# Gates as tanh, merge tiles ahead of the silu tiles, squares on VectorE and four modulation blocks on TensorE in a two-block kernel

## The reference

```python
z = rms_norm(x, norm_g) @ w_in            # 20 pieces, the last is mg: 4 x 1024 wide
y_a = fox_attention(...)                  # 8 heads, causal
y_b = rg_lru(xb, ...)                     # r, i = sigmoid(gates); a = exp(-8 r softplus(-lam)); scan
y_c = nsa_attention(...)                  # compressed, selected and window attention
y_d = spatial_gating(ud, vd, ...)
ys = [y_a * silu(ga), y_b * silu(gb), y_c * silu(gc), y_d * silu(gd)]
merged = sum_n sigmoid(mg[n]) * (ys[n] @ w_branch[n])
out = x + merged @ w_out
```

## Time and profile before

| | us |
|---|---|
| median of 3 runs | 1929.52 (1928.55 to 1930.72) |
| the profiled execution | 1932.03 |
| its span in the trace | 1930.3 |
| TensorE busy | 1719.5 (89%) |
| TensorE weight loads | 1457.5 (76%) |
| VectorE busy | 1350.7 (70%) |
| ScalarE busy | 901.9 (47%) |

### The profile page before, as it was taken

One profiled execution on the slowest core, in us unless ns is written; L12 is line 12 of the kernel. 1 busy time (PEld: TensorE's weight loads), 2 busy tenths in 40 slices (PEclk: granted clock), 3 DMA queues, 4 the chain that ended last, 5 costly groups with the idle time before them and its releaser, 6 DMA issues. The chain is left out here.

```text
span 1930.3 us, 26100 instructions
## 1 busy us (share of the span) xinstructions
PE 1719.5 (89%) x10016; PEld 1457.5 (76%) x10016; DVE 1350.7 (70%) x2526; ACT 901.9 (47%) x1535; POOL 48.4 (3%) x113
## 2 busy tenths in 40 slices
PE   2699998668999998988899898999997998999997
PEld 0578876456788886867688776888896887888987
DVE  7677873447799999867995477389964444655585
ACT  2533333625444442226464465333344575796741
POOL 0800000000000000000000000000000000000000
PEclk8799999879999998999999899999998989899999
DMA  7333331003222325653463101354554443433542
GB/s 278 128 131 110 131 128 47 1 33 131 70 95 88 106 91 176 218 165 101 158 209 130 55 1 66 110 166 152 154 187 142 148 147 121 121 121 112 161 144 98
DMA packets 65348, 237.93 MB, mean 123 GB/s; under 512 B 7183, under 2 KB 8648, under 8 KB 64968
## 3 DMA queue, kind: packets, MB, share of 16 engines
q1 hardware_dynamic: 64456, 234.69, 37.2%
q10 hardware_dynamic: 768, 1.58, 0.2%
HBM read 234.93 MB, written 1.05 MB: 122 GB/s over the span
## 5 line engine op out<-in xcount | busy, mean ns | idle before, releaser
L442 PE MATMUL banks<-m,weights_high 128*128 128x256 f32 (+1 forms) x4336 | 1050.5, 336 | 104.2 <-DVE m L871 45.1
L442 PEld LDWEIGHTS banks<-m,weights_high 128*128 128x128 f32 x4336 | 744.6, 194 | 201.5 <-DVE m L871 48.0
L442 PE MATMUL banks<-m,weights_low 128*128 128x256 f32 (+1 forms) x2168 | 720.3, 332 | 0.0
L474 DVE TENSOR_TENSOR weights_low<-weight_ring,weights_high 128x1024 fp32r<-128x1024 f32 x294 | 357.4, 1223 | 287.8 <-ACT weights_high L469 286.8
L442 PEld LDWEIGHTS banks<-m,weights_low 128*128 128x128 f32 x2168 | 420.6, 194 | 38.8
L469 ACT ACTIVATE weights_high<-weight_ring 128x1024 fp32r<-128x1024 f32 x294 | 310.2, 1056 | 283.6 <-PE banks L442 234.4
L591 DVE SCALAR_TENSOR_TENSOR m<-m,columns 128x189 f32<-128x189 f32 (+4 forms) x856 | 321.5, 452 | 22.6 <-ACT m L543 22.3
L716 DVE SCALAR_TENSOR_TENSOR m<-weight_ring,m 128x1024 bf16<-128x1024 f32 x192 | 234.7, 1223 | 16.4 <-DMA weight_ring<-in_weights 9.6
L542 ACT ACTIVATE m<-banks,columns 128x512 f32<-128x512 f32 (+1 forms) x120 | 83.3, 694 | 307.6 <-PE banks L442 307.4
L442 PE MATMUL banks<-m,weight_ring 128*128 128x256 f32 x704 | 155.2, 384 | 2.4 <-ACT m L833 2.4
L442 PEld LDWEIGHTS banks<-m,weight_ring 128*128 128x128 f32 x704 | 135.8, 193 | 21.8 <-ACT m L833 2.8
(11 more groups left out here) (363 smaller groups left out, 1629.1 us busy)
## 6 DMA issues: line engine op xcount, KB each, us to landing
weight_ring<-in_weights SPq DMA_DIRECT2D x434, 512.0 KB, 3.6
x<-in_tokens SPq DMA_DIRECT2D x1, 2048.0 KB, 14.3
m<-in_cmp_w SPq DMA_DIRECT2D x1, 2048.0 KB, 7.5
m<-in_cond SPq DMA_DIRECT2D x2, 512.0 KB, 4.9
out<-x SPq DMA_DIRECT2D x1, 1024.0 KB, 4.8
columns<-in_columns SPq DMA_DIRECT2D x1, 633.0 KB
m<-in_rg_w ACTq DMA_DIRECT2D x1, 512.0 KB, 4.5
m<-in_spatial_w ACTq DMA_DIRECT2D x1, 512.0 KB
```

The lines of the kernel that those rows point to most:

```text
L442: mm = pe.matmul(out, lhsT, rhs, start=p.start and i == 0, stop=p.stop and i == len(passes) - 1)
L474: dve.tensor_tensor(w_lo[:, g % PARTS, :], K.ring[:, PLACE[PRODUCT_BLOCKS[g]] % RING, :], w_hi[:, g % PARTS, :].bitcast(F32), ALU.subtract ...
```

## The change

- Setup: the first four mod0 blocks are laid out transposed and formed on TensorE as products of a 128x128 tile and two columns (`Modulator.sum`); they are spread among the other twelve in the stream. VectorE forms twelve blocks, then adds the bias to the four. A small transfer with the transposed conditions goes ahead of the others.
- Start of a stage: what VectorE makes first for `Normalise` (where the root is known before the stage) and `Split` goes ahead of the low parts of the weights (`vector_first`).
- `project2`: mg is emptied with Tanh (scale 0.5) instead of Sigmoid and comes ahead of ga: mg 35 to 66, ga 67 to 70, gb 71 to 74, gc 75 to 78, gd 79 to 82. The merge uses (tanh + 1) and a factor 0.5. The gates of the recurrence become Tanh as well, one item later; the scratch of the side branches moves to ga to gd. Attention results are stored to tiles of their own, and VectorE multiplies each silu tile when it is emptied. Attention pairs come every 7 ticks.
- The squares of the four sets go to VectorE. The key root becomes Ln and Exp, and each root and the forget logarithms load one table that holds both. Some slots move by one item.

```diff
+MOD_PE = 4
+SQUARES_AT = 2
-STREAM = blocks_of("mod0")[:MOD_FIRST] + blocks_of("even_in")[:TOGETHER] \
+STREAM = spread_among(blocks_of("mod0")[:MOD_PE], blocks_of("mod0")[MOD_PE:MOD_FIRST]) + blocks_of("even_in")[:TOGETHER] \
...
+            if prepare:
+                prepare.vector_first(dve)
             for g in range(begun, n_ahead):
                 low_part(dve, g)
...
+        sync.dma_start(self.turned, self.K.dram["cond_t"]).then_inc(*self.K.conds.up(16))
...
+    def sum(self, pe, b):
+        K, j = self.K, b - FIRST_TILE["mod0"] // TPB
+        pe.wait_ge(*K.silued.at(1))
+        wait_loaded(K, pe, PLACE[b])
+        for k in range(KD):
+            mm = pe.matmul(K.bank[:, 0, 2 * j:2 * j + 2], K.ring[:, PLACE[b] % RING, k * P:k * P + P],
+                           self.turned[:, k, :], start=k == 0, stop=k == KD - 1)
+        mm.then_inc(*K.mod_summed.up())
...
+            for b in on_tensor[:SQUARES_AT]:
+                modulator.sum(pe, b)
             pe.wait_ge(*ones.at(1))
             for k in range(KD):
                 sums.add(pe, k)
+            for b in on_tensor[SQUARES_AT:]:
+                modulator.sum(pe, b)
...
+            modulator.take_sums(dve, MOD_PE)
...
+        for name, branch in (("ga", self.attention.forgetting), ("gb", self.side.xc), ("gc", self.attention.selected),
+                             ("gd", self.f["ud"])):
+            j = item - self.item_of[name]
+            if 0 <= j < KB:
+                dve.wait_ge(*emptied)
...
+                gate = self.f[name][:, j, :]
+                dve.tensor_tensor(gate, gate, branch[:, j, :], ALU.mult)
...
-    BEGIN, SPACING = 62, 8
+    BEGIN, SPACING = 62, 7
...
-            dve.tensor_tensor(f[name][:, j, :], f[name][:, j, :], K.bank[:, self.OUT, 0:LAT],
-                              ALU.mult).then_inc(*self.gated.up())
+            kept = self.selected if branch else self.forgetting
+            dve.tensor_copy(kept[:, j, :], K.bank[:, self.OUT, 0:LAT]).then_inc(*self.stored.up())
...
-    KEYS, KEY_SQUARE, VALUES, KEY_SUM, KEY_ROOT, KEY_SCALE = 14, 15, 15, 17, 18, 20
+    KEYS, KEY_SQUARE, VALUES, KEY_SUM, KEY_ROOT, KEY_SCALE = 15, 16, 16, 18, 19, 21
...
-            act.activation(self.sq, f[self.SETS[i][0]], ACT.Square).then_inc(*self.squared.up())
...
+            act.preload_act_table_set(LOG_EXP)
             rt = self.rt.rearrange("p (b a) t -> p b (a t)", a=2)
             rsqrt(act, Link(act, self.scalar_step), rt, K.bank[:, 4:6, :], K.small[:, 0:1], 1.0 / HD).then_inc(
...
+            dve.tensor_tensor(self.sq, whole, whole, ALU.mult).then_inc(*self.squared.up())
...
-            act.activation(self.r[:, j, :], K.bank[:, self.BANK, 0:LAT], ACT.Sigmoid, bias=K.col("b_rg_a", j), scale=1.0)
+            act.activation(self.r[:, j, :], K.bank[:, self.BANK, 0:LAT], ACT.Tanh, bias=self.halves[:, 0, j:j + 1], scale=0.5)
...
-        if u == self.OUTPUT:
-            dve.tensor_tensor(f["gb"], f["gb"], xc, ALU.mult).then_inc(*self.output.up())
...
-                        return dve.tensor_tensor(total, bank[:, 0:LAT], f["mg"][:, b * KD + n, :], ALU.mult)
-                    link(dve.tensor_tensor(tmp, bank[:, 0:LAT], f["mg"][:, b * KD + n, :], ALU.mult))
+                        return dve.scalar_tensor_tensor(total, tanh, 1.0, bank[:, 0:LAT], ALU.add, ALU.mult)
+                    link(dve.scalar_tensor_tensor(tmp, tanh, 1.0, bank[:, 0:LAT], ALU.add, ALU.mult))
...
-                        link(dve.tensor_copy(merged_hi[:, n, :], total))
-                        ins = dve.tensor_tensor(merged_lo[:, n, :], total, merged_hi[:, n, :].bitcast(F32), ALU.subtract)
+                        link(dve.tensor_scalar(merged_hi[:, n, :], total, 0.5, None, ALU.mult))
+                        ins = dve.scalar_tensor_tensor(merged_lo[:, n, :], total, 0.5, merged_hi[:, n, :].bitcast(F32),
+                                                       ALU.mult, ALU.subtract)
```

More of the change, by code:

```diff
@@ L692, in __init__, with plan_tensor @@
         self.unread = K.take(D, dtype=BF16)
+        self.turned = K.take(KD, 2)
         self.planned = K.mod_done.total
+    def plan_tensor(self, blocks):
+        for i, b in enumerate(blocks):
+            self.K.release[PLACE[b]] = (self.K.mod_summed.sem, i + 1)
     def plan(self, blocks):
@@ L717, in block, with take_sums @@
                                      ALU.mult, ALU.mult, accum_out=K.mod[:, layer, j, c:c + 1]).then_inc(*K.mod_done.up())
+    def take_sums(self, dve, n):
+        K = self.K
+        dve.wait_ge(*K.mod_summed.now())
+        m = K.mod[:, 0, 0:n, :]
+        dve.tensor_tensor(m, K.bank[:, 0, 0:2 * n].rearrange("p (j c) -> p j c", c=2), last(K.col("mod_b0", 0, n), 2),
+                          ALU.add)
     def end(self, dve, blocks):
@@ L842, in scalar, with lead, norm, begin @@
             high_part(KD - 1)
-    def vector(self, dve):
-        K, t0 = self.K, self.t0
+    def lead(self):
+        return 3 if self.plain is None else KD
+    def norm(self, dve, k):
+        K = self.K
+        x = K.x[:, k, self.t0:T]
+        if self.shift_scale:
+            ins = dve.tensor_tensor(self.place[k], x, self.rstd, ALU.mult)
+        else:
+            ins = dve.scalar_tensor_tensor(self.place[k], x, K.col(self.gain, k), self.rstd, ALU.mult, ALU.mult)
+        ins.then_inc(*self.normed.up())
+    def begin(self, dve):
+        K = self.K
         if self.shift_scale:
@@ L851, in vector, with vector_first @@
             ins.then_inc(*self.scaled.up())
[L853 to L859, removed]
         if self.known is None:
             dve.wait_ge(*self.rooted.at(1))
-        lead = 3 if self.plain is None else KD
-        for k in range(lead):
-            norm(k)
+        for k in range(self.lead()):
+            self.norm(dve, k)
+    def vector_first(self, dve):
+        if self.known is not None:
+            self.begin(dve)
+    def vector(self, dve):
+        if self.known is None:
+            self.begin(dve)
         for k in range(KD if self.plain is None else 0):
-            if k + lead < KD:
-                norm(k + lead)
+            if k + self.lead() < KD:
+                self.norm(dve, k + self.lead())
             hi, lo = self.parts[k]
@@ L2281 @@
 IN2 = [("kc", 1, "Copy"), ("vc", 1, "Copy"), ("qc", 4, "Copy"), ("kd", 4, "Copy"), ("qa", 4, "Copy"), ("ka", 4, "Copy"),
[L2282 to L2283 removed]
+       ("xb", 4, "Copy"), ("ud", 4, "Gelu"), ("mg", 32, "Tanh"), ("ga", 4, "Silu"), ("gb", 4, "Silu"), ("gc", 4, "Silu"),
+       ("gd", 4, "Silu")]
 def hybrid_layer(K, out):
@@ L2314, in project2 @@
     rounds, tile, item_of, item = [], first, {}, 0
-    func_of = {"Copy": ACT.Copy, "Gelu": ACT.Gelu, "Silu": ACT.Silu, "Sigmoid": ACT.Sigmoid}
+    func_of = {"Copy": ACT.Copy, "Gelu": ACT.Gelu, "Silu": ACT.Silu, "Tanh": ACT.Tanh}
     def h(k):
@@ L2489, in weigh @@
             if begins and p:
-                pe.wait_ge(*self.gated.at(p if not branch else KB + j))
+                pe.wait_ge(*self.stored.at(p if not branch else KB + j))
             for e in range(2):
@@ L2758, in scalar @@
             act.wait_ge(*self.key_summed.at(1))
-            act.activation(self.krt.rearrange("p g c -> p (g c)"), K.bank[:, 6, 2 * P:2 * P + 2 * NC], ACT.Sqrt,
-                           bias=K.small[:, 0:1], scale=1.0 / HD).then_inc(*self.key_rooted.up())
+            act.preload_act_table_set(LOG_EXP)
+            rsqrt(act, Link(act, self.scalar_step), self.krt.rearrange("p g c -> p (g c)"),
+                  K.bank[:, 6, 2 * P:2 * P + 2 * NC], K.small[:, 0:1], 1.0 / HD).then_inc(*self.key_rooted.up())
         if u == self.EXP:
@@ L2788, in vector @@
         live, sums, peak = self.live, self.sums, self.peak
+        i = self.set_at(u, self.SQUARE)
+        if i is not None:
+            dve.wait_ge(*emptied)
+            if i:
+                dve.wait_ge(*self.summed.at(i))
+            whole = f[self.SETS[i][0]]
+            dve.tensor_tensor(self.sq, whole, whole, ALU.mult).then_inc(*self.squared.up())
         i = self.set_at(u, self.SCALE)
```

98 lines of the change are left out of this document (59 added, 39 removed).

## The result

| | before | after |
|---|---|---|
| median, us | 1929.53 (1928.55 to 1930.72) | 1909.66 (1907.43 to 1916.41) |
| ratio | | 0.9905, 95% 0.9883 to 0.9926 |
| profiled execution, span | 1932.0, 1930.3 | 1916.4, 1914.7 |
| forecast | | 1896, range 1885 to 1910 |

The change gives 20 us where I forecast 33. The median lies just inside the stated range, and outside the forecast's own range of 1889 to 1903. The two profiled executions differ by 15.6 only, because the one after lies 6.7 above its median and the one before 2.5 above its own. First the page's busy times of the changed kernel, then two stretches, setup and `project2`.

A forecast was written before the change was run, and what follows sets the result against it. Each changed place was priced by its own limit: VectorE in setup and merge, TensorE with its waits in project2. 9.2 + 1.7 + 23.1 - 0.4 - 0.3 = 33.3 us gained, giving 1896 us, range 1885 to 1910.

The forecast's parts named there:

- Setup: Setup: four blocks fewer on VectorE save 10.6 us; less 0.5, 0.2 and 0.7, 9.2 us gained.
- the ring: Setup: late release of places on TensorE delays later transfers, so VectorE loses 0.7 us.
- place 15: Setup: transfer issued when place 10 is released at 36.1, landing at 40.0; VectorE wants it at 39.3.
- Seam: Start of the stage after setup: first normalised tiles go ahead, TensorE begins 7.2 us after the start; 1.7 us gained.
- Tables: project2, ScalarE: 54 table loads become 23, taking away 39.8 us, and four squares 4.2; no gain in itself.
- The named waits: project2, TensorE: waits of 3.64, 3.41 and 2.58 us go, 9.6 together; of the 1.44 wait, 1.3 is gained.
- Seven waits of 0.25 to 0.80: project2, TensorE: small waits, 3.9 us together, are halved, gaining 2.0, as new ones appear.
- fourth rival: project2: pairs every 7 ticks bunch and every pair waits, 72 us lost against 33 gained; 1935 us, chance 0.04.
- The clock: project2: half clock around the three large waits ends with them, 1.7, 5.1 and 3.4; 10.2 us gained.
- Merge: Merge, where VectorE sets the time: new operand forms and the rounding cost 0.3 us, at most 2.7.
- first rival: project2: waits did not hang on ScalarE's time, half rate returns, 10 gained instead of 23.1; 1909 us, chance 0.13.
- upper bound of 36: project2: most the stage could gain, all idle time but the start and all clock loss, 36 us.

The follow-up runs named there:

- e5: The kernel before run again, nothing edited, for its trace; project2 357.0 us, no whole time given.
- e13: Changed kernel with its new 64-byte tile taken last in the setup's memory, so later tiles lie as in the kernel before; 1908.6 us, ratio 0.9896.
- e6: Changed kernel, pairs still every 7 ticks, second head's transposes and the copy behind them one tick later; 1900.84 us, ratio 0.9874.
- e2: Changed kernel with pairs every 8 ticks instead of 7 and gc and gd exchanged; 1905.46 us, ratio 0.9881.
- e9: Kernel before with 64 unused bytes per partition reserved ahead of the modulator's memory, shifting all later tiles; ratio 1.0003.
- e1: Changed kernel run again, nothing edited; 1908.8 us, ratio 0.9904.
- e15: Changed kernel with second head's transposes one tick later, new tile in the first projection's scope, 192 bytes at the second feed-forward; 1895.82 us, ratio 0.9832.
- e16: The kernel of e15 with the mixing gate's products over 128 columns instead of 24; 1898.13 us, ratio 0.9835.
- e7: Changed kernel with the mixing gate's products over all 128 columns instead of 24; ratio 0.9903.
- e14: Changed kernel run a third time, nothing edited; 1907.29 us, ratio 0.9896.

## Why the forecast was too fast, step by step

- **Setup: right within 1.1, with one term mis-sized.** 8.1 for 9.2. The first block was 0.8 late, not 0.5, and the ring cost 0.87 and 1.22, not 0.7. A sum on TensorE was taken as 1.5 us, from eight records; it has 16 and took 3.5 for each of the first two blocks and 1.8 for the others. With it the squares ended at 35.9, forecast 34.6, and VectorE had place 15 at 41.2, forecast 40.0.
- **Seam: right.** The first product 7.0 after the stage's start, forecast 7.2; 1.9 for 1.7.
- **Tables: right.** 23 loads are left, as counted, and ScalarE's time fell by 44 (39.8 and 4.2 forecast). None of it was time by itself.
- **The named waits: right, all gone**, 3.64, 3.41, 2.58, 1.44.
- **"Seven waits of 0.25 to 0.80 ... half, 2.0, as new ones will appear with pairs every 7 ticks": the first step that failed.** New ones appeared, but 8.2 us of them at the transposes. Between the traces in one layout (e5 and e13) idle time fell by 4.1, forecast 12.9. This is the fourth rival's place at a small price: I had written against it that "the 5 ticks are unchanged", which holds for the first head and not for the second head's transposes, whose distance to the first head's copy is spacing less six. e6 shows this for the ticks' part; for the waits on the division nothing was taken apart.
- **"The clock ... I take all of it", 10.2: the second.** The three stretches did go, but 3.4 came back behind the wait of 2.88 (e2 and e6 remove it), and the loss at the gate's narrow products grew from 4.4 to 6.8. In the layout of before (e13) it grew to 5.1 only: 0.7 is the wait of 1.44 turned into work at half clock, and for the other 1.7 no cause is shown. Also, 5.3 of the 19.4 lost in the trace that I read was that execution's: its repetition lost 14.1 with the same waits, and 4.9 instead of 10.2 in the three stretches that I had summed. (The Trainium skill, page "TensorE: Matmul & The Clock Gate", section "What's actually happening", has the number of slow matmuls at a kernel's start vary between runs of one kernel. In these traces the same shows behind waits in its midst: 5.1 and 1.5 us behind one and the same wait.)
- **What stood in no step: the layout.** Within `project2` the 64 bytes took 7.1, more than a third of the miss of 17 there; in the total they cost nothing, as e9 and e13 show from both sides. So they explain the stage and not the time. This is in part why the 20 us are more than the steps give: 8.1 + 1.9 + 5.7 - 0.3 = 15.4. In e1 against the first trace of before, stages that the change does not touch are 5.7 shorter in sum: the first projection, apart from the seam, by 3.4, the scan and its output product by 2.2, the second feed-forward by 2.6, the other output product by 1.1; the first feed-forward is 2.4 longer and the mLSTM stage 0.9.
- **Merge: right**, 0.3 lost. The new form, one operand from the bank and a constant, takes 414 to 418 ns (busy time by count of L3084, L3085).

The time that came is the first rival's, 1909. Its mechanism was so in one half only: the half clock came back, but the waits did not return in their old places; the change's own spacing made those on the copy. That its number came out so close is partly luck: it has `project2` gain 10, where 5.7 were measured (7.3 in one layout), and stages of which it does not speak gave the rest.

The fourth rival's sum is wrong as it stands in the prediction: 72 us lost against 33 gained is 39 slower, 1968 and not 1935. And the stage's upper bound of 36, all idle and all clock, fits only with the 10.2 us of the three stretches; with the 19.4 that the stage lost it would be about 45.

In one layout, then, (e5 to e13) `project2` gave 7.3 of 22.7. Of the 15.4 missing, 8.8 are idle time, 6.3 clock, 0.3 work.

## What to carry to other kernels

When a schedule in ticks is made denser, list every pair of steps whose distance is the spacing less a constant; those shrink, and one tick there was worth 6.6 us of a stage in which the whole change gained 5.7. A stretch at half clock in one trace is not a fixed price of the wait before it: read two executions before you sum them. And an edit that adds one small persistent tile moves all the others: compare TensorE's work at full clock, stage by stage, before you look for waits.

## What the runs showed that I had not expected

- **TensorE's pace at full granted clock depends on where the moving tile lies.** Triples of 256 columns took 0.340 to 0.360 us, of 512 columns 0.681 to 0.700. By the tile's start modulo 512 bytes (as the built programs lay it out), with the weight parts on 128 in all runs: 256 columns 0.360 on 128 and 384, 0.353 on 192 and 448, 0.350 on 160, 0.340 to 0.354 on 64; 512 columns 0.681 on 384, 0.682 on 128, 0.687 on 448, 0.698 on 0, 0.700 on 64. The place is not all: on 64 the second feed-forward of e15 kept 0.353, and that of e16, whose tiles lie the same and whose edit is in another stage, ran at 0.340 to 0.346. What the rule is stays open. The Trainium skill, page "TensorE: Matmul & The Clock Gate", section "Back-to-back issue gap", has for an isolated matmul of N columns a spacing of N/2.4 + 2.5 ns at the full clock, by which a triple of 256 would be an estimated 0.328 us. Every one measured here is longer.
- **24 columns cost nearly as much as 256.** In e1, at full clock, a matmul of 24 columns follows the last after 0.111 us, one of 256 after 0.120. The half clock begins among the narrow ones, in both kernels, and e7, with 128 columns there, loses 3.3 us instead of 6.8.
- **The mLSTM stage, which nothing touches, has different lengths**, 66.8 to 68.4 us in some executions and 69.7 to 71.0 in others. Its idle time and its work at full clock are the same in e1 and e14 (23.2 and 23.3, 35.7 and 35.7), and the clock loss is 11.7 and 8.0. The clock at its begin tells them apart: the first 9 us of these two executions of the changed kernel:

```profile
317.20:326.20 9.00, 7.89 (x10) 0.52 0.00 0
```

```profile
316.50:325.50 9.00, 4.89 (x11) 0.97 0.00 0
```

Between e1 and e14 this is 3.7 of the 4.3 us by which their spans differ, as large as several of the effects sought here. It is not all of the scatter: the first trace of the changed kernel is 4.8 longer than e1, and 0.4 of that is here. Why the clock differs at the stage's begin is not known.
